# Loading x and the first weights through one DMA queue, and another order for the first 30 products of a two-layer convolutional trunk

## What is computed

```
def swiglu(x, w_gate, w_up, w_down):
    return (jax.nn.silu(x @ w_gate) * (x @ w_up)) @ w_down
for i in range(DEPTH):
    x = x + FFN_RES_WEIGHT * swiglu(rms_norm(x, ffn1_norm[i]), ffn1_w_gate[i], ffn1_w_up[i], ffn1_w_down[i])
    hn = rms_norm(x, mix_norm[i])
    ...
    x = x + m
    x = x + FFN_RES_WEIGHT * swiglu(rms_norm(x, ffn2_norm[i]), ffn2_w_gate[i], ffn2_w_up[i], ffn2_w_down[i])
return rms_norm(x, final_norm), ...
```

## Time and profile before

| what | us |
|---|---|
| median of 3 runs (2396.0 to 2396.76) | 2396.59 |
| the profiled execution's own time | 2395.2 |
| its span on the slowest core, core 4 | 2393.3 |
| span of the fastest core, core 2 | 2391.0 |
| PE busy (share of the span) | 2342.4 (98%) |
| DVE, ACT, POOL busy | 937.2, 579.0, 444.7 |
| first matmul of an item, core 4 | 16.52 |
| first down product, core 4 | 139.10 |

### The profile page before, as it was taken

The page is one execution under the profiler, slowest core; times in us unless marked ns, Lnnn a source line. Parts: engine busy times, 40 slices in busy tenths (PEclk is TensorE's granted clock), DMA queues, the critical chain, the costliest instruction groups (busy, mean ns, idle before and its releaser), DMA issues.

```text
span 2393.3 us, 33594 instructions; the slowest of 8 cores (2391.0 to 2393.3 us)
## 1 busy us (share of the span) xinstructions
PE 2342.4 (98%) x14211; PEld 1292.8 (54%) x14211; DVE 937.2 (39%) x1613; ACT 579.0 (24%) x1037; POOL 444.7 (19%) x463
## 2 busy tenths in 40 slices
PE   6899999999999999999999999999999999999997
PEld 2455555555544555555555555555555555555554
DVE  2342232274477342232262423324655733224226
ACT  3401101242376201101241011013322330110124
POOL 1310000250466000000240000004300510000015
PEclk9899999999999999999999999999999999999999
DMA  9152332327500432332222423232333244223224
GB/s 172 44 71 27 41 48 36 36 32 169 108 2 5 58 45 34 44 38 36 36 36 27 54 36 45 27 44 28 46 40 35 27 49 49 36 36 45 33 30 142
DMA packets 189878, 116.44 MB, mean 49 GB/s; under 512 B 8224, under 2 KB 188576, under 8 KB 189728
## 3 DMA queue, kind: packets, MB, share of 16 engines
q0 software_dynamic: 166464, 83.90, 29.4%
q1 hardware_dynamic: 22848, 29.76, 4.5%
q10 hardware_dynamic: 416, 0.64, 0.1%
HBM read 183.29 MB, written 14.88 MB: 83 GB/s over the span
## 4 chain that ended last, share of the span: by engine, by line
PE 94%; DVE 2%; DMA 1%; ACT 1%; POOL 0%; issue 0%; SPq 0%; DVEq 0%; ACTq 0%; POOLq 0%
PE ps L586 25%; PE ps L625 25%; PE ps L580 25%; PE ps L1109 7%; PE ps L1232 2%; PE ps L752 2%; PE ps L746 2%; PE ps L993 2%; PE ps L935 2%; DMA arena<-ffn_w_up 1%; DVE arena L461 1%; PE ps L839 0%; DVE arena L877 0%; DMA arena<-xT 0%; ACT L449 0%
## 5 line engine op out<-in xcount | busy, mean ns | idle before, releaser
L580 PE MATMUL ps<-arena 128*128 128x412 bf16 (+1 forms) x3520 | 698.2, 340 | 14.7 <-DVE arena L461 14.1
L586 PE MATMUL ps<-arena 128*128 128x412 bf16 (+1 forms) x3520 | 692.7, 340 | 4.9 <-DMA arena<-ffn_w_up 4.9
L597 DVE TENSOR_TENSOR arena<-arena,ps 128x412 bf16<-128x412 f32 (+1 forms) x440 | 256.8, 584 | 944.7 <-ACT arena L595 944.6
L625 PE MATMUL ps<-arena 128*128 128x412 bf16 (+1 forms) x3520 | 618.8, 338 | 0.0
L595 ACT ACTIVATE arena<-ps 128x412 f32<-128x412 f32 (+1 forms) x440 | 226.0, 514 | 1369.1 <-PE ps L586 1368.9
L580 PEld LDWEIGHTS ps<-arena 128*128 128x128 bf16 x3520 | 344.3, 98 | 298.9 <-DVE arena L461 29.8
L586 PEld LDWEIGHTS ps<-arena 128*128 128x128 bf16 x3520 | 346.1, 98 | 278.8 <-issue 12.0
L625 PEld LDWEIGHTS ps<-arena 128*128 128x128 bf16 x3520 | 343.7, 98 | 270.5
L628 DVE SCALAR_TENSOR_TENSOR arena<-ps,arena 128x412 f32<-128x412 f32 (+1 forms) x480 | 280.3, 586 | 242.4 <-PE ps L625 242.1
L402 POOL TENSOR_TENSOR arena<-arena 128x412 f32<-128x412 f32 (+3 forms) x229 | 243.6, 1064 | 213.9 <-ACT arena L394 194.8
L461 DVE SCALAR_TENSOR_TENSOR arena<-arena,ps 128x412 bf16<-128x412 f32 (+3 forms) x280 | 170.3, 636 | 94.6 <-ACT ps L454 94.6
(11 more groups left out here) (78 smaller groups left out, 777.5 us busy)
## 6 DMA issues: line engine op xcount, KB each, us to landing
arena<-ffn_w_gate POOLq DMA_DIRECT2D x44, 512.0 KB, 8.7
arena<-ffn_w_up POOLq DMA_DIRECT2D x44, 512.0 KB, 10.4
arena<-ffn_w_down POOLq DMA_DIRECT2D x32, 512.0 KB, 9.5
yT<-arena SPq DMA_DIRECT2D x16, 412.0 KB, 3.7
arena<-ffn_w_down POOLq DMA_DIRECT2D x16, 384.0 KB, 8.1
arena<-a_w_pw POOLq DMA_DIRECT2D x12, 512.0 KB, 13.0
arena<-b_w_in POOLq DMA_DIRECT2D x12, 512.0 KB, 9.5
vb<-arena SPq DMA_DIRECT2D x8, 512.0 KB, 5.6
```

The lines of the kernel that those rows point to most:

```text
L580: P.emit("pe", (lambda e, k=k, jj=jj, t0=t0, w=w, bg=bg, wgv=wgv: e.matmul(psum[:, bg, 0:w], wgv[:, k, jj * 128:(jj + 1) * 128], XN[:, k, ...
L586: pk = P.emit("pe", (lambda e, k=k, jj=jj, t0=t0, w=w, bu=bu, wuv=wuv: e.matmul(psum[:, bu, 0:w], wuv[:, k, jj * 128:(jj + 1) * 128], XN[: ...
L597: dd = P.emit("dve", (lambda e, s=s, w=w, bu=bu, hj=hj, t0=t0: e.tensor_tensor(out=HB[:, hj, t0:t0 + w], in0=ST[:, s, 0:w], in1=psum[:, bu ...
L625: pk = P.emit("pe", (lambda e, jj=jj, mm=mm, t0=t0, w=w, b=b, wdv=wdv, n=n: e.matmul(psum[:, b, 0:w], wdv[:, jj, mm * 128:(mm + 1) * 128], ...
```

## The change

Six parts:

1. All pieces of the tiles 1 to 4 of x are issued by POOL, in one queue with the weights and in this order: g0, u0, x1, g2, u2, x2, g4, u4, x3, x4. None of them waits for another. Tile 0 and the constants stay on SP.
2. The gate on the weights moves: before, u0 (unit 1) waited for the third piece of tile 0, and g0 for nothing; now g0 waits for the second piece of tile 0.
3. Tile 1 comes in 2 pieces (before 4) and tile 2 in 2 (before 1). `wq`, used only much later, waits for tile 4.
4. The items are in another order: (0,0), (1,0); normalize tile 1; (0,1), (1,1), (2,0), (3,0); normalize tile 2; (2,1), (3,1); (0,2) to (3,2); (4,0), (5,0), (4,1), (5,1), (4,2), (5,2); then tiles 3 and 4 as before. The ScalarE and VectorE parts of the first two items are held back until tile 1 is normalized.
5. Tile 2 is normalized as tiles 0 and 1 are, by `pieces_in`, and no longer by POOL's additions.
6. The squares and sums of the tiles 3 and 4 come at other places of the order.

```diff
-                gate = [ld_x[0, 2]] if v == 1 else []
+                gate = [ld_x[0, 1]] if v == 0 else []
...
-    X_PIECES = [4, 4, 1, 1, 1]
+    X_PIECES = [4, 2, 2, 1, 1]
...
-    load_x(0, None)
+    load_x(0, "sp")
     c_tk = P.emit("sp", lambda e: e.dma_start(out=CONST, in_=consts), sem="ld_c", amount=16)
-    W.topup()
-    load_x(1, W.load_tk[3])
-    load_x(2, x_tk[1])
-    load_x(3, x_tk[2])
-    load_x(4, None)
+    for ti in range(1, NT):
+        if ti < 4:
+            W.topup(limit=2 * ti)
+        load_x(ti, "pool")
...
+        norm_in(0)
+        need(0)
+        acquire(0)
+        waiting = [products(hj, 0) for hj in (0, 1)]
+        norm_in(1)
+        need(1)
         for it in waiting:
             gate(*it)
-        order = [(hj, ti) for ti in (1, 2) for hj in range(6)]
+        acquire(2)
+        acquire(4)
+        order = [(0, 1), (1, 1), (2, 0), (3, 0), (2, 1), (3, 1)]
+        order += [(hj, 2) for hj in range(4)] + [(hj, ti) for ti in range(3) for hj in (4, 5)]
         order += [(2 * jp + j, ti) for jp in range(3) for ti in (3, 4) for j in range(2)]
-        squares = {0: (2, 0), 1: (2, 4), 6: (3, 0), 7: (3, 4), 8: (4, 0), 9: (4, 4)}
-        sums = {3: 2, 9: 3, 11: 4}
+        squares = {7: (3, 0), 9: (3, 4), 10: (4, 0), 12: (4, 4)}
+        sums = {12: 3, 14: 4}
         for i, (hj, ti) in enumerate(order):
             gate(*products(hj, ti))
+            if i == 3:
+                norm_in(2)
```

More of the change, by code:

```diff
@@ L262, in plan, with topup @@
             self.units.append((src, shape, tag))
-        def topup(self):
-            while self.next_dma < len(self.units) and self.free_slots:
+        def topup(self, limit=None):
+            while self.next_dma < (limit or len(self.units)) and self.free_slots:
                 v = self.next_dma
@@ L347, in build_program, with load_x @@
     xsrc = xT.rearrange("(c p) t -> p c t", p=128)
-    def load_x(ti, gate):
+    def load_x(ti, eng):
         t0, w = TILES[ti]
@@ L352, in load_x @@
         for j in range(X_PIECES[ti]):
-            x_tk[ti] = ld_x[ti, j] = P.emit("sp", (lambda e, t0=t0, w=w, c0=j * n, c1=(j + 1) * n: e.dma_start(
-                out=X[:, c0:c1, t0:t0 + w], in_=xsrc[:, c0:c1, t0:t0 + w])), waits=[gate], sem="ld_x%d_%d" % (ti, j), amount=16)
-    load_x(0, None)
+            x_tk[ti] = ld_x[ti, j] = P.emit(eng, (lambda e, t0=t0, w=w, c0=j * n, c1=(j + 1) * n: e.dma_start(
+                out=X[:, c0:c1, t0:t0 + w], in_=xsrc[:, c0:c1, t0:t0 + w])), sem="ld_x%d_%d" % (ti, j), amount=16)
+    load_x(0, "sp")
     c_tk = P.emit("sp", lambda e: e.dma_start(out=CONST, in_=consts), sem="ld_c", amount=16)
-    W.topup()
-    load_x(1, W.load_tk[3])
-    load_x(2, x_tk[1])
-    load_x(3, x_tk[2])
-    load_x(4, None)
+    for ti in range(1, NT):
+        if ti < 4:
+            W.topup(limit=2 * ti)
+        load_x(ti, "pool")
     def x_ld(ti, c):
         return ld_x[ti, c * X_PIECES[ti] // KC]
-    wq_tk = P.emit("sp", lambda e: e.dma_start(out=WQF, in_=wq), sem="ld_wq", amount=16)
+    wq_tk = P.emit("sp", lambda e: e.dma_start(out=WQF, in_=wq), waits=[x_tk[4]], sem="ld_wq", amount=16)
     ones_tk = P.emit("dve", lambda e: e.memset(ONES, 1.0))
@@ L523, in start_group, with norm_in @@
         nrm.ring = view(O_CB, [8, 512], F32)
[L524 to L537, removed]
+        nrm.accb = {3: view(O_RS + 3072, [512], BF16)}
+        def norm_in(ti):
+            nrm.pieces_in(ti)
+            nrm.rstd(ti)
+            for c in range(KC):
+                later.append((nrm, ti, c))
+        norm_in(0)
[4 more added lines that the diff above has]
+        need(1)
         for it in waiting:
             gate(*it)
-        order = [(hj, ti) for ti in (1, 2) for hj in range(6)]
+        acquire(2)
+        acquire(4)
+        order = [(0, 1), (1, 1), (2, 0), (3, 0), (2, 1), (3, 1)]
+        order += [(hj, 2) for hj in range(4)] + [(hj, ti) for ti in range(3) for hj in (4, 5)]
         order += [(2 * jp + j, ti) for jp in range(3) for ti in (3, 4) for j in range(2)]
-        squares = {0: (2, 0), 1: (2, 4), 6: (3, 0), 7: (3, 4), 8: (4, 0), 9: (4, 4)}
-        sums = {3: 2, 9: 3, 11: 4}
+        squares = {7: (3, 0), 9: (3, 4), 10: (4, 0), 12: (4, 4)}
+        sums = {12: 3, 14: 4}
         for i, (hj, ti) in enumerate(order):
             gate(*products(hj, ti))
+            if i == 3:
+                norm_in(2)
             if i in squares:
```

## The result

| what | before | changed |
|---|---|---|
| median of 5 runs each, us | 2396.59 | 2380.29 |
| the profiled execution's own time | 2395.2 | 2380.29 |
| span of its slowest core | 2393.3 (core 4) | 2378.5 (core 5) |
| first down product, latest core / mean of 8 | 139.10 / 138.15 | 124.43 / 122.25 |
| span, mean of 8 | 2392.5 | 2376.1 |

The ratio is 0.9929, with a 95% interval of 0.9917 to 0.994: faster by 16.3 us, where 16.9 was forecast. In some runs of every kernel here the cores of a die show a lower granted clock and take longer (one of the five of the changed kernel took 2704.59 us); the times of the experiments leave those runs out, but their ratios still hold some runs of the kernel before of 2414 to 2419 us.

The account below looks back on a forecast made before the run. TensorE, busy 98% of the span, bounds the kernel, so only time before the first down product can be won: step by step it comes at 122.2 instead of 139.1 us, 2396.6 - 16.9 = 2379.7 us, range 2373 to 2388.

Parts of the forecast that it names:

- The first item: Start of the stage: g0, now behind tile 0's second piece, lands and the first item starts at 15.0 us (14 to 16.5).
- no weight unit is waited for: Sign to look for in the new trace: TensorE waits for no weight unit, with x1's second piece there at 24 us.
- Tile 1: After (1,0): x1 lands at 23.9 us, no table load follows the sums, and tile 1's first item starts at 29.5.
- (0,1): Tile 1's first item takes 6.5 us as before, to 36.0; (1,1), (2,0) and (3,0) follow at 2.79 each.
- Tile 2's gap: New stall behind (3,0): Silu, squares and sums take 6.1 us, to 50.5; then (2,1) at the slow pace takes 5.5.
- Tiles 3 and 4: Last twelve items, 33.6 us: squares come early enough, leaving only lags of 1.0 and 0.6 us from VectorE's last multiplies.
- The margin of POOL: Tiles 3 and 4: seven POOL additions take 8.30 us, so tile 4's end about 3 us before its sum is needed.
- Nothing behind: From the first down product on, nothing is paid: TensorE runs at full clock and everything moves as a block.
- Rival A: Loads of x: POOL's queue charges the weights' packet price, 10.3 us a tile; gain 12.3 us, 2384.3; chance 0.17.
- Rival B: Whole stage a bit better: g0 at 14, x1 irrelevant, clock back behind tile 2, no later lag; gain 22.7, 2373.9; chance 0.18.
- Rival C: Tiles 3 and 4: their waits return because squares and POOL's additions end late; gain 5.8 us, 2390.8; chance 0.08.
- Rival D: Tile 1's sums: slower if x1 lands from 45.6 us on, the stage ending 98.3 behind it; chance 0.03 with its like.

Follow-up runs that it names:

- e3: The changed kernel with g0 issued at once, without its wait for tile 0: 2378.5 us, ratio 0.9908 to the kernel before.
- e6: The changed kernel with x1 behind g2 and u2 in the POOL queue instead of ahead of them: 2387.1 us (one run).
- e4: The changed kernel with squares and sums of tiles 3 and 4 as close before their first items as before the change: 2391.8 us, ratio 0.9954.
- e8: The changed kernel with tiles 1 to 4 of x on SP, each waiting for the weight unit it follows: 2391.7 us, ratio 0.9977.

## Why the prediction was right

The sum gave 122.2 us for the first down product and the profiled core has 122.90; the total followed, 2379.7 against 2380.29. The mechanisms held. That the end came within 0.7 us is in part luck, since steps that were up to 2.4 us late were made up by others that were priced too high. By its steps, in us from the start of the span:

| step | forecast | core 5 |
|---|---|---|
| first item | 15.0 | 16.52 |
| (1,0) done | 25.2 | 27.18 |
| tile 1's first item | 29.5 | 30.72 |
| (0,1) done | 36.0 | 37.66 |
| (3,0) done | 44.4 | 46.80 |
| (2,1) starts | 50.5 | 51.91 |
| (2,1) done | 56.0 | 55.19 |
| (0,3) starts | 86.7 | 87.14 |
| first down product | 122.2 | 122.90 |

1. **The first item** was mis-sized by 1.5 us on this core, and by 2.2 on the mean of the eight (17.2). I had let g0 gain some of what tile 0 gains. It does not: on five of the eight cores the first item started between 17.6 and 18.9 us, where before it was 16.4 to 17.8. Holding g0 back delivers tile 0 earlier to an engine that then waits for g0; e3 shows that both orders end at the same place. Nor did the sign hold that no weight unit is waited for: u0 was waited for 1.08 us on core 5, and 0.4 to 2.2 on six others.
2. **Tile 1** was right in its mechanism: 1.99 us from sums to matmul with no table load. It was also right that x1's landing and TensorE's own two items meet within a microsecond there: the sums ran as eight in a row at 27.18, at once behind (1,0), so on this core it was TensorE that was late, while on cores 1, 3, 4 and 6 the last sums waited 0.45 to 2.36 us for the squares of x1. x1 itself was 1.7 us later than forecast (25.57 for 23.9), about as much as g0. e6 shows what a late x1 costs: all of its delay.
3. **(0,1)** took 6.94 us, not 6.5: all eight matmuls of its up product came at the slow pace (34.92 to 37.66), where before the pace rose among them (53.29 to 55.61). (1,1) lost another 0.8 us in the same way.
4. **Tile 2's gap** was right in place and cause, and 1.0 too long (5.1 for 6.1): squares of four chunks take 1.58 us, 3.03 for two, not twice 1.8, and the last four sums 1.35, not 1.7. The slow pace behind it was overstated by more, 3.28 us for (2,1) instead of 5.5. These two errors, 3.2 us, more than cancel the 2.4 by which (3,0) was late. One cost was missing: VectorE's last chunks of tile 2 come late for (0,2) as well, 0.9 us (57.98 to 60.31 for its eight gate matmuls). The total was nearer than its parts, by luck.
5. **Tiles 3 and 4**: 1.2 and 1.0 us of lag for 1.0 and 0.6, with the mechanism as forecast. The margin of POOL was overrated: its additions for tile 4 end at 85.62 and their sum runs at 86.96, 1.3 us later and not 3. e4 puts a number on the reason: 11.9 us when the squares and sums stand as close to their items as they stood.
6. **Nothing behind** the stage: from its first down product to its end a core takes 2253.1 to 2255.0 us in all twelve traces, as means of the eight cores.

Rival A, a price for x in POOL's queue, is out. The DMA view of the changed kernel's core 5 from 45 to 50 us, when only x is left in that queue:

```profile
q0 software_dynamic: 407, 1.62, 104.0%
```

0.324 MB per us, a little above the 0.297 of SP's queue in the earlier trace rows. The Trainium skill's rule in "DMA: Bandwidth & Descriptors", section "Issuing engine by pattern", that a simple load belongs on SyncE, would have spoken against the change; here x on SP (e8) was 12 us slower than x among GpSimd's weights. That is no measurement of the path itself, since e8 also issues x1 later and lets it share the engines with g2 to u4; what counted was x1's place among the weights. Rival B's better clock came true behind tile 2's gap for 2.2 of its 2.7 us and made up for the late start; the rest of rival B did not come. Rival C was the right thing to fear and is now priced. Rival D's sensitivity, one for one, is what e6 measured; the landing was never near 45.

What stays open: what g0's wait is worth, since its effect is below what these runs tell apart; what the number of pieces (part 3) does, which no run changes by itself; and whether x1 from SP without the wait for u0 would come as early as from POOL's queue.

## What to carry to other kernels

When a stage waits for several loads, write the loads and the work down as one order of use, and price them together: here the halves alone were worth minus 10 and plus 1 us of the stage, and both 16. Put every step that only prepares a later tile (squares, sums, Ln and Exp) as many items ahead of its first use as its slowest chain is long, on every engine that it crosses: taking it back at tiles 3 and 4 cost 12 of the 16 us, and two items' lead for one ScalarE step gave 3 more. And compute a wait in front of data from the bytes that must be there, not from the order in which two needed loads are issued.

## What the runs showed of the hardware

Plain float32 rows of x went through POOL's queue as packets of 4.0 KB on average (1.62 MB in 407), where SP's queue had cut them to 1.6 KB (0.89 MB in 545); I had feared 512 B. Per byte the two queues are about equal, 0.324 and 0.297 MB per us. When both had work in e8, they moved packets one for one (499 and 503 in 5 us), so that the queue with the longer packets moved more bytes, 0.80 MB to 0.25. And a load from SP beside a busy POOL queue started late: on every core of e8, x1's first packet came 3 to 5 us after its issue, where x2 of the kernel before, issued at 40.51 on idle engines, had moved its first by 42.
